# Experts' last product in three parts, with its weights split by VectorE

## The chip, the cores and the metric

The kernel runs on one core of a Trainium2 chip. The metric is the device time of one execution in microseconds (us), as the median of several runs. Engines are named as in the profile: PE (TensorE), PEld (its weight loads), DVE (VectorE), ACT (ScalarE), POOL (GpSimd), SP (SyncE, which here only issues DMAs).

## The reference

One transformer block on 2048 tokens of width 1024: a mixer of three kinds of attention, a mixture of experts, a gated embedding, and a norm. The change touches the last two.

```
def expert_block(inp):                      # one block of 128 tokens, one of 32 experts
    xb, e = inp
    hmid = jax.nn.silu(xb @ w_gate[e]) * (xb @ w_up[e])      # 1024 -> 512
    return hmid @ w_down[e]                                  # 512 -> 1024
...
h = h + hier_moe(rms_norm(h, g_ffn[i]), ...)
e = rms_norm(p[i] @ w_ple[i], g_ple[i])
h = h + e * jax.nn.sigmoid(h @ w_ple_gate[i])                # 1024 -> 1024
return rms_norm(h, g_final)
```

Each token goes to two experts. The tokens of an expert are padded to blocks of 128, so that an expert has one or more blocks; with these inputs 48 blocks are computed.

## The kernel before

The stages follow one another, each in a block of its own that starts when all engines have finished the one before: projections and the choice of keys, the mixers, the output product, routing (`route`), the experts (`experts`), and the last part (`finish`). All are written out by hand: each engine has its own list of instructions, in order, and waits on semaphores.

**Experts.** Every weight matrix of an expert is 2 MB, and one DMA loads it. Gate and up weights have two places (`low`, by the parity of the expert), and so have the down weights (`wd`). Gate and up products are made in three parts: a float32 matrix is split into `high`, its value cast to the type fp32r, and `low`, the rest, and PE adds high·high, high·low and low·high, three matmuls of 128x512 for each of the 8 slices of the inner dimension (L2361 to L2363). DVE makes the weights' parts, by halves of 128x2048: a cast (L2269) and a subtraction (L2271), so 4 pairs for an expert. `high` has one place for the gate and one for the up weights, so DVE's gate pairs of the next expert wait for the last gate product of this one (`g_done`), its up pairs for the last up product (`u_done`). POOL subtracts to make the low part of the turned input (`split_x`, L2296), ACT its high part (L2421). The down product (L2379) takes plain float32 operands, 8 matmuls of 128x512 per block, and each shows as two records.

PE's order in the loop, for block b: gate product of b+1, turning of the hidden values of b (`turn_h`, L2370), up product of b+1, turning of the input of b+2 (`turn_x`, L2349), down product of b (L2379). Below, these are G, H, U, X and Y. ACT: silu of b+1, copy of the turned hidden values of b (`copy_h`, L2439), copy of up, copies of the turned input, output of b. POOL: the gather of the input of b+2 (L2287, L2288), its list of rows (L2281), the product silu x up (`hidden`, L2302), the two subtractions of `split_x`. SP, for expert e from 2 on: wait for the last G of e-2, load gate (L2165); wait for the last U, load up; wait for the last Y, load down (L2170). The next expert's gate load stands behind that in SP's order.

**The last part.** While the experts run, SP loads the gate weights of the last part into a place of their own (`wg`) and DVE casts them into `low`'s even place once its expert pairs are done (L2275). When `finish` begins, DVE first subtracts to get their low part (L2765, 8 instructions), then adds the experts' results to h (L2727) and makes the low part of the turned h (L2736). ACT first squares and copies the embeddings of the first three tiles (L2681, L2683), then copies the turned h (L2690). PE turns and multiplies those embeddings (L2627, L2637), turns h (L2615) and makes the gate product in three parts (L2651 to L2653) for 16 tiles.

Of the kernel before, what the change touches and what calls it, by code (L numbers as in the profile page):

```python
# [1859 lines left out]
def route(nc, outer, router, slots, gates, rows, blocks, ident, prefetch, p, w_ple, room, e_dram, e_squares, f_dram, xb, x_loaded):  # L1860
# [5 lines left out]
    with ExitStack() as ctx:  # L1866
# [38 lines left out]
        emb, pt = room[:, 0:4, :], room[:, 4:8, :].rearrange("p a (b n) -> p (a b) n", n=PLE)  # L1905
# [247 lines left out]
GATE, UP = 0, 1  # L2153


def expert_weights(nc, outer, low, wd):
# [3 lines left out]
    return low, wd, gu_loaded, outer.enter_context(nc.semaphore("p7_d_loaded"))  # L2160
# [19 lines left out]
def experts(nc, outer, f_dram, weights, w_gate, w_up, w_down, gathers, y_dram, blocks, ident, load_next, load_tail, wg, wg_high, wg_loaded):
# [3 lines left out]
    with ExitStack() as ctx:  # L2186
# [9 lines left out]
        low, wd, gu_loaded, d_loaded = weights  # L2196
# [22 lines left out]
        hT_turned, hT_done = sem("hT_turned"), sem("hT_done")  # L2219
# [10 lines left out]
        def _(sp):  # L2230
# [26 lines left out]
        def _(dve):  # L2257
            with dve.Fori(0, NE // 2) as it:
                for par in range(2):
# [3 lines left out]
                    for m, done in ((GATE, g_done), (UP, u_done)):  # L2263
                        dve.wait_ge(gu_loaded[m][par], it * 16 + 16)

                        dve.wait_ge(done, once)
                        for half in range(2):
                            k = slice(half * HK, (half + 1) * HK)
                            dve.tensor_copy(high[:, m, k, :], low[:, par, m, k, :].bitcast(F32)).then_inc(high_done, 1)  # L2269
                            dve.wait_ge(high_done, e * 4 + (2 * m + half + 1))  # L2270
                            dve.tensor_tensor(low[:, par, m, k, :], low[:, par, m, k, :].bitcast(F32), high[:, m, k, :].bitcast(F32), ALU.subtract).then_inc(w_split, 1)  # L2271

            for k in range(KD):
                dve.wait_ge(wg_loaded, 16 * KD)
                dve.tensor_copy(wg_high[:, k, :], wg[:, k, :]).then_inc(wg_split, 1)  # L2275
            dve.wait_ge(wg_split, KD)

        @block.gpsimd
        def _(pool):
# [18 lines left out]
            def hidden(b, par):  # L2298
# [3 lines left out]
                pool.tensor_tensor(hid[:, par, :], act_g[:, :], act_u[:, :], ALU.mult).then_inc(h_done, 1)  # L2302
# [7 lines left out]
            hidden(0, 0)  # L2310
            split_x(1)
            m = rounds(pool)
            with pool.Fori(0, m) as it:
                for par in range(2):
# [4 lines left out]
                    hidden(b + 1, 1 - par)  # L2319
                    split_x(b + 2)  # L2320
            hidden(m * 2 + 1, 1)
# [8 lines left out]
        def _(pe):  # L2330
# [35 lines left out]
            def turn_h(b, par):  # L2366
                pe.wait_ge(h_done, b + 1)
                pe.wait_ge(hT_done, b + 1)
                for k in range(KF):
                    mm = pe.transpose(psH[:, k * P:(k + 1) * P], hid[:, par, k * P:(k + 1) * P], ident[:, :])  # L2370
                mm.then_inc(hT_turned, 1)

            def down(b, par, e, at):
                pe.wait_ge(hT_done, b + 2)
                pe.wait_ge(d_loaded, e * 16 + 16)
                for c in range(2):
                    pe.wait_ge(y_copied[c], b + 1)
                    for k in range(KF):
                        mm = pe.matmul(psY[:, c, :], hT[:, par, k, :], wd[:, bass.ds(at, 1), k, c * CH:(c + 1) * CH].rearrange("p a f -> p (a f)"),  # L2379
                                       start=k == 0, stop=k == KF - 1)  # L2380
# [8 lines left out]
            with pe.Fori(0, m) as it:  # L2389
                for par in range(2):  # L2390
# [3 lines left out]
                    turn_h(b, par)  # L2394
# [3 lines left out]
                    down(b, par, e, at)  # L2398
# [3 lines left out]
            turn_h(b, 0)  # L2402
            product(b + 1, UP, e, at)
            e, at = expert(b)
            down(b, 0, e, at)
            turn_h(b + 1, 1)
            e, at = expert(b + 1)
            down(b + 1, 1, e, at)

        @block.scalar  # L2410
        def _(act):
# [24 lines left out]
            def copy_h(b, par):  # L2436
                act.wait_ge(hT_turned, b + 2)
                act.wait_ge(y_done, b * 2 + 2)
                act.activation(hT[:, par, :, :], psH[:, :].rearrange("p (k t) -> p k t", t=P), ACT.Copy).then_inc(hT_done, 1)  # L2439
# [15 lines left out]
            with act.Fori(0, m) as it:  # L2455
                for par in range(2):
                    b = it * 2 + par
                    silu(b + 1)
                    copy_h(b, par)
# [5 lines left out]
            copy_h(b, 0)  # L2465
            copy_u(b + 1)
            output(b, 0, m)
            copy_h(b + 1, 1)
# [3 lines left out]
def finish_weights(nc, outer, ctx):  # L2472
# [9 lines left out]
    wg, first_h = sb("p8_wg", [KD, D]), sb("p8_first_h", [D])  # L2482
    low, wd = sb("p7_low", [2, 2, KD, FE], F32R), sb("p7_wd", [2, FE // P, D])
    return (wg, first_h, low, wd), (sem("w_loaded"), sem("h_loaded0"), sem("tail_loaded"))


def split_places(weights):
    low = weights[0][2]
    return [low[:, i, :, :, :].rearrange("p m k f -> p (m k f)").rearrange("p (k n) -> p k n", n=D) for i in range(2)]


def tail_places(weights):

    wd = weights[0][3]
    return (wd[:, 0, 0:2, :], wd[:, 0, 2, 0:OWN * PLE].rearrange("p (j n) -> p j n", n=PLE), wd[:, 0, 3, :],
            wd[:, 1, 0, :], wd[:, 1, 1, :], wd[:, 1, 2, 0:2 * KP * P].rearrange("p (b k t) -> p b k t", b=2, k=KP))


def load_finish_weights(sp, weights, w_pg, h_dram):
    (wg, first_h, _, _), (w_loaded, h_loaded, _) = weights  # L2500
    for k in range(KD):
        sp.dma_start(wg[:, k, :], w_pg[0, k * P:(k + 1) * P, :]).then_inc(w_loaded, 16)
    sp.dma_start(first_h[:, :], h_dram[0:P, :]).then_inc(h_loaded, 16)


def load_tail(sp, weights, p, w_ple, g_ple):
    wp, ptail, gp, _, _, _ = tail_places(weights)
# [3 lines left out]
    sp.dma_start(gp, row_broadcast(g_ple, D)).then_inc(tail_loaded, 16)  # L2511
    sp.wait_ge(w_loaded, 16 * KD)
    sp.wait_ge(h_loaded, 16)
    sp.wait_ge(tail_loaded, 48)


def finish(nc, outer, h_dram, y_dram, rows, gates, e_dram, e_squares, weights, blocks, g_final, out, ident):

    with ExitStack() as ctx:  # L2519
# [7 lines left out]
        (wg, first_h, low_gu, _), (_, h_loaded0, _) = weights  # L2527
        wg_high, wg_low = split_places(weights)
        wp, ptail, gp, second_h, gf, pT = tail_places(weights)
        ht = [first_h[:, :], second_h]  # L2530
        half = sb("half", [P, 1])
        e, y1, y2 = sb("e", [P, NS, D]), sb("y1", [P, NS, D]), sb("y2", [P, NS, D])
        hT_high, hT_low = sb("hT_high", [P, 2, KD, P], F32R), sb("hT_low", [P, 2, KD, P], F32R)

        sg, result, junk = wg[:, 0:2, :], wg[:, 2:4, :], wg[:, 4, :]
# [22 lines left out]
        def _(sp):  # L2558
# [9 lines left out]
            load_h(1)  # L2568
            load_h(2)
# [38 lines left out]
        def _(pe):  # L2608
# [11 lines left out]
            second = pe.snap((first + 1) % 2)  # L2620
# [19 lines left out]
            def product(t, halves=(0, 1)):  # L2640
# [5 lines left out]
                for c in halves:  # L2646
                    for k in range(KD):
                        if (t, c) == (0, 0):
                            pe.wait_ge(w_split, k + 1)
                        w_high, w_low = (low_gu[:, bass.ds(i, 1), k // 4, k % 4 * 2 + c, :].rearrange("p a f -> p (a f)") for i in (first, second))  # L2650
# [66 lines left out]
        def _(dve):  # L2717
# [46 lines left out]
            for k in range(KD):  # L2764
# [17 lines left out]
def hybrid_block_kernel(nc, x, p, rel_bias, g_mix, w_in, gla_w_alpha, gla_b_alpha, gla_g_norm, swa_sinks, w_out, g_ffn,  # L2782
# [14 lines left out]
    with ExitStack() as outer:  # L2797
# [17 lines left out]
        with ExitStack() as ctx:  # L2815
            ple = finish_weights(nc, outer, ctx)
            (wg, _, low, wd), (wg_loaded, _, _) = ple
            with ExitStack() as ffn:
                weights = expert_weights(nc, outer, low, wd)
                gathers = first_gathers(nc, outer, ffn, router)  # L2820

                def prefetch(sp, e_copied):
# [8 lines left out]
                route(nc, outer, router, gathers[0], gates, rows, blocks, ident, prefetch, p, w_ple, wg, e_dram, e_squares, f_dram, gathers[1], gathers[2])  # L2831
                experts(nc, outer, f_dram, weights, w_expert_gate, w_expert_up, w_expert_down, gathers, y_dram, blocks, ident,
                        lambda sp: load_finish_weights(sp, ple, w_ple_gate, h_dram), lambda sp: load_tail(sp, ple, p, w_ple, g_ple),
                        wg, split_places(ple)[0], wg_loaded)
            finish(nc, outer, h_dram, y_dram, rows, gates, e_dram, e_squares, ple, blocks, g_final, out, ident)
# [24 lines left out]
```

## Time and profile before

| | |
|---|---|
| three runs | 2977.5, 2985.3, 2990.5 us; median 2985.3 |
| the profiled execution | 2976.7 us, of which the span is 2975.0 us |
| routing ends, experts begin | at about 1771 us of the span |
| experts end, last part begins | 2746 to 2754 us |
| PE busy over the span | 2673.1 us (90%) |
| DVE busy | 1818.3 us (61%) |
| POOL busy | 952.3 us (32%) |

An engine's busy share is a mean over stages with different limits. Times in the trace are microseconds from the start of the span. The row of a timeline gives start, duration, engine, line, operation, tile written <- tiles read, how many are merged in the row, and in brackets how long the engine had been idle before and what ended that.

### The profile page before, as it was taken

What the parts mean: (1) busy time and instruction counts of PE and PEld (TensorE: products, weight loads), DVE (VectorE), ACT (ScalarE), POOL (GpSimd) and SP (SyncE); (2) the same over time, 40 slices, a digit from 0 to 9 for tenths busy, and PEclk for the clock granted to TensorE, in tenths of its full rate; (3) what the DMA queues carried; (4) which work ended last, traced back from release to release, by engine and by line L of the source; (5) the groups of instructions that cost most, each with busy time, mean ns of one, the idle gap of its engine ahead of it and who ended that gap; (6) DMA issues with size and microseconds to landing.
All of it is one profiled execution on the core that took longest, in us unless ns stands there. A gap on an engine that the chain in (4) does not pass through costs nothing. (4 is left out here: it accounts for less than half of the span.)

```text
span 2975.0 us, 34899 instructions
## 1 busy us (share of the span) xinstructions
PE 2673.1 (90%) x11088; PEld 1675.0 (56%) x11089; DVE 1818.3 (61%) x2274; ACT 1279.4 (43%) x2369; POOL 952.3 (32%) x935
## 2 busy tenths in 40 slices
PE   6989889999957878878799888999999999998998
PEld 3634333444843444444588746666666666665687
DVE  2187999688886756776322367764564445741676
ACT  2377878839805566665322142222222222222322
POOL 1477887200011111120000014543444334531321
PEclk9999999999977989999799899999999999999999
DMA  5102221111141122222544377996596655982563
GB/s 152 55 30 53 31 38 40 54 56 56 40 128 43 62 66 74 70 81 66 179 148 149 123 268 261 339 352 216 204 342 219 219 213 204 344 298 82 194 216 135
DMA packets 221746, 438.61 MB, mean 147 GB/s; under 512 B 23032, under 2 KB 91192, under 8 KB 221496
## 3 DMA queue, kind: packets, MB, share of 16 engines
q1 hardware_dynamic: 199384, 357.26, 35.0%
q0 software_dynamic: 13456, 47.85, 5.1%
q10 hardware_dynamic: 8784, 31.99, 2.6%
q8 instruction: 63, 1.03, 0.1%
q14 instruction: 59, 0.48, 0.0%
HBM read 331.14 MB, written 105.91 MB: 147 GB/s over the span
## 5 line engine op out<-in xcount | busy, mean ns | idle before, releaser
L2269 DVE CAST p_high<-p_low 128x2048 fp32r<-128x2048 f32 x128 | 203.1, 1587 | 407.6 <-PE p_psG L2363 292.8
L626 PE MATMUL p_psP<-home,p_ring 128*128 128x512 f32 (+1 forms) x960 | 420.6, 597 | 0.0
L2379 PE MATMUL p_psY<-p_wd,p_hT 128*128 x768 | 339.7, 596 | 2.2 <-ACT p_hT L2439 1.9
L2271 DVE TENSOR_TENSOR p_low<-p_low,p_high 128x2048 fp32r<-128x2048 f32 x128 | 319.9, 2499 | 4.4
L626 PEld LDWEIGHTS p_psP<-home,p_ring 128*128 128x128 f32 (+1 forms) x960 | 175.4, 185 | 239.6 <-issue 239.4
L2379 PEld LDWEIGHTS p_psY<-p_wd,p_hT 128*128 128x128 f32 x768 | 143.0, 191 | 164.8 <-issue 164.7
L2302 POOL TENSOR_TENSOR p_hid<-p_act_g,p_act_u 128x512 f32<-128x512 f32 x48 | 62.7, 1306 | 526.5 <-ACT p_act_u L2434 274.2
L2296 POOL TENSOR_TENSOR p_xT_low<-p_xT,p_xT_high 128x512 fp32r<-128x512 f32 x96 | 189.6, 1994 | 4.0 <-ACT p_xT L2424 4.0
L655 PE MATMUL p_psI<-p_kI,p_qI 64*128 64x512 f32 (+3 forms) x608 | 146.0, 587 | 48.7 <-ACT p_relu L551 48.5
L2361 PE MATMUL p_psG<-p_high,p_xT_high 128*128 128x512 f32 x384 | 170.2, 443 | 15.7 <-DVE p_low L2271 8.1
L699 DVE TENSOR_SCALAR_CACHE_REDUCE p_equal<-p_S_low,p_flip 128x512 uint8<-128x512 f32 (+4 forms) x139 | 168.7, 1213 | 0.0
L2361 PE MATMUL p_psU<-p_high,p_xT_high 128*128 128x512 f32 x384 | 157.8, 411 | 5.9 <-DVE p_low L2271 5.9
L565 ACT ACTIVATE p_relu<-p_relu,p_small 128x512 f32<-128x512 f32 (+3 forms) x266 | 161.5, 662 | 0.0
L2445 ACT ACTIVATE p_y<-p_psY 128x512 f32<-128x512 f32 x96 | 57.4, 598 | 226.7 <-PE p_psY L2379 226.7
L2362 PE MATMUL p_psG<-p_low,p_xT_high 128*128 x384 | 153.1, 399 | 0.0
L2363 PE MATMUL p_psG<-p_high,p_xT_low 128*128 128x512 f32 x384 | 152.8, 398 | 0.0
L551 ACT ACTIVATE p_relu<-p_psI 128x1024 f32<-128x1024 f32 (+3 forms) x152 | 136.7, 914 | 37.1 <-PE p_psI L655 12.6
L699 DVE TENSOR_SCALAR_CACHE_REDUCE p_above<-p_S_low,p_flip 128x384 uint8<-128x384 f32 (+4 forms) x139 | 150.6, 1083 | 3.3
L2362 PE MATMUL p_psU<-p_low,p_xT_high 128*128 x384 | 152.0, 396 | 0.0
L2363 PE MATMUL p_psU<-p_high,p_xT_low 128*128 128x512 f32 x384 | 151.9, 396 | 0.0
L1331 PE MATMUL p_psL<-p_kA,home 64*128 64x512 f32 (+3 forms) x320 | 86.6, 617 | 67.9 <-ACT home L1217 33.3
L1474 DVE SCALAR_TENSOR_TENSOR p_logits<-p_mask,p_psL 128x1024 f32<-128x1024 uint8 (+3 forms) x80 | 84.8, 1060 | 100.6 <-PE p_psL L1331 100.5
(397 smaller groups left out, 5592.7 us busy)
## 6 DMA issues: line engine op xcount, KB each, us to landing
p_low<-in_w_expert_gate_dram SPq DMA_DIRECT2D x32, 2048.0 KB, 13.5
p_low<-in_w_expert_up_dram SPq DMA_DIRECT2D x32, 2048.0 KB, 18.1
p_wd<-in_w_expert_down_dram SPq DMA_DIRECT2D x32, 2048.0 KB, 10.7
y_dram<-p_y ACTq DMA_DIRECT2D x48, 512.0 KB, 8.2
p_xt<-in_x_dram SPq DMA_DIRECT2D x32, 512.0 KB, 4.4
y_dram<-p_clear SPq DMA_DIRECT2D x32, 512.0 KB, 4.5
proj_f<-p_stage SPq DMA_DIRECT2D x52, 256.0 KB, 2.3
p_ot<-o_dram SPq DMA_DIRECT2D x16, 512.0 KB, 4.3
```

Of the source, the lines that this page charges most:

```text
L551: act.activation(relu[:, n % NRELU, :, 0:c1 - c0], psI[:, n % NI, :, 0:c1 - c0], ACT.Relu).then_inc(relu_done, 1)
L565: act.activation(dst, src, ACT.Copy, scale=small[:, j, h:h + 1]).then_inc(weighed, 1)
L626: mm = pe.matmul(psP[0:n, i % 2, :], w, aT[:, k, c * CH:(c + 1) * CH], start=k == 0, stop=k == KD - 1)
L655: mm = pe.matmul(psI[:, n % NI, half, 0:c1 - c0], qI[r, b % 2, i, :], kI[r, c0:c1], start=True, stop=True)
L699: return dve.tensor_scalar((above, equal)[jj % 2][:, 0:W], scores_of(S_low, S_high, j), value, None, ALU.is_ge, ALU.add, accum_out=cnt[:, ...
L2269: dve.tensor_copy(high[:, m, k, :], low[:, par, m, k, :].bitcast(F32)).then_inc(high_done, 1)
L2271: dve.tensor_tensor(low[:, par, m, k, :], low[:, par, m, k, :].bitcast(F32), high[:, m, k, :].bitcast(F32), ALU.subtract).then_inc(w_split, 1)
L2296: pool.tensor_tensor(xT_low[:, k, :], xT[:, k, :], xT_high[:, k, :].bitcast(F32), ALU.subtract).then_inc(xT_split, 1)
L2361: pe.matmul(ps[:, :], xT_high[:, k, :], high[:, m, k, :], start=k == 0, stop=False)
L2362: pe.matmul(ps[:, :], xT_high[:, k, :], left, start=False, stop=False)
L2363: mm = pe.matmul(ps[:, :], xT_low[:, k, :], high[:, m, k, :], start=False, stop=k == KD - 1)
L2379: mm = pe.matmul(psY[:, c, :], hT[:, par, k, :], wd[:, bass.ds(at, 1), k, c * CH:(c + 1) * CH].rearrange("p a f -> p (a f)"), start=k == 0 ...
```

## The change

The down product is made in three parts too. The down weights get a high and a low place for each parity (`down`, which takes the room of `wd` and of the last part's `wg`); DVE splits them after the up weights of the same expert. ACT writes the turned hidden values twice (`hT_high`, `hT`), POOL subtracts to get `hT_low` (`split_h`, ahead of `hidden` in its order), and Y waits for both splits. `hid`, `hT` have one place each instead of two, so `copy_h` of b waits for Y of b-1. The last part's gate weights are loaded in two halves into `low`'s even place when the last expert but one has left it, and DVE splits them there, into `down`'s even place and in place, after the last expert's weights; `finish` no longer subtracts. Its other tiles move into the odd places; g_ple is loaded at the start of `finish`. In routing, the first down load goes ahead of the second expert's gate load.

```diff
@@ load_down @@
-    sp.dma_start(wd[:, par, :, :], ...).then_inc(d_loaded, 16)
+    sp.dma_start(down[:, par, LOW_PART, :, :].bitcast(F32), ...).then_inc(d_loaded, 16)
@@ experts: sync @@
-            load_next(sp)
...
-            twice = sp.snap(used * 2 + 4)
-            sp.wait_ge(y_done, twice)
+            once = sp.snap(used + 1)
+            for m, done in ((GATE, g_done), (UP, u_done)):
+                sp.wait_ge(done, once)
+                sp.wait_ge(w_split, 4 * (NE - 2) + 2 * m + 2)
+                load_gate_half(sp, m)
+            used = sp.value_load(blocks[0:1, NBX + 2 + NE:NBX + 3 + NE], min_val=0, max_val=NBLK)
+            once = sp.snap(used + 1)
+            sp.wait_ge(u_done, once)
             load_tail(sp)
@@ experts: vector, after the gate and up pairs of expert e @@
+                    dve.wait_ge(d_loaded, e * 16 + 16)
+                    for half in range(2):
+                        k = slice(half * KF // 2, (half + 1) * KF // 2)
+                        dve.tensor_copy(down_w[:, par, HIGH, k, :], down_w[:, par, LOW_PART, k, :].bitcast(F32)).then_inc(d_high, 1)
+                        dve.wait_ge(d_high, e * 2 + (half + 1))
+                        dve.tensor_tensor(down_w[:, par, LOW_PART, k, :], down_w[:, par, LOW_PART, k, :].bitcast(F32), down_w[:, par, HIGH, k, :].bitcast(F32), ALU.subtract).then_inc(d_split, 1)
+            dve.wait_ge(y_done, twice)
             for k in range(KD):
-                dve.wait_ge(wg_loaded, 16 * KD)
-                dve.tensor_copy(wg_high[:, k, :], wg[:, k, :]).then_inc(wg_split, 1)
+                dve.wait_ge(wg_loaded, 16 * 2)
+                dve.tensor_copy(wg_high[:, k, :], wg[:, k, :].bitcast(F32)).then_inc(wg_split, 1)
+                dve.wait_ge(wg_split, 2 * k + 1)
+                dve.tensor_tensor(wg[:, k, :], wg[:, k, :].bitcast(F32), wg_high[:, k, :].bitcast(F32), ALU.subtract).then_inc(wg_split, 1)
@@ experts: gpsimd @@
+            def split_h(b):
+                pool.wait_ge(hT_done, b + 2)
+                pool.tensor_tensor(hT_low[:, :, :], hT[:, :, :], hT_high[:, :, :].bitcast(F32), ALU.subtract).then_inc(hT_split, 1)
...
-                pool.wait_ge(hT_turned, b)
+                pool.wait_ge(hT_turned, b + 1)
...
                     load_slots(b + 3, 1 - par)
-                    hidden(b + 1, 1 - par)
+                    split_h(b)
+                    hidden(b + 1)
                     split_x(b + 2)
@@ experts: tensor, down @@
-                pe.wait_ge(hT_done, b + 2)
-                pe.wait_ge(d_loaded, e * 16 + 16)
+                pe.wait_ge(hT_split, b + 1)
+                pe.wait_ge(d_split, e * 2 + 2)
...
-                        mm = pe.matmul(psY[:, c, :], hT[:, par, k, :], wd[...], start=k == 0, stop=k == KF - 1)
+                        pe.matmul(psY[:, c, :], hT_high[:, k, :], w_high, start=k == 0, stop=False)
+                        pe.matmul(psY[:, c, :], hT_high[:, k, :], w_low, start=False, stop=False)
+                        mm = pe.matmul(psY[:, c, :], hT_low[:, k, :], w_high, start=False, stop=k == KF - 1)
@@ experts: scalar, copy_h @@
-                act.wait_ge(y_done, b * 2 + 2)
-                act.activation(hT[:, par, :, :], psH[...], ACT.Copy).then_inc(hT_done, 1)
+                act.wait_ge(y_done, b * 2 + 4)
+                act.activation(hT_high[:, :, :], src, ACT.Copy)
+                act.activation(hT[:, :, :], src, ACT.Copy).then_inc(hT_done, 1)
@@ finish: sync, vector @@
+            sp.dma_start(gp, row_broadcast(g_ple, D)).then_inc(gp_loaded, 16)
...
-            for k in range(KD):
-                dve.tensor_tensor(wg_low[:, k, :], wg[:, k, :], wg_high[:, k, :].bitcast(F32), ALU.subtract).then_inc(w_split, 1)
             add(0)
             low(0)
             add(1)
+            dve.wait_ge(gp_loaded, 16)
@@ prefetch, in routing @@
-                    for e in range(2):
-                        load_gate_up(sp, weights, GATE, e, e, w_expert_gate)
-                        if e == 1:
-                            sp.wait_ge(e_copied, NT - OWN - 4)
-                        load_gate_up(sp, weights, UP, e, e, w_expert_up)
-                    load_down(sp, weights, 0, 0, w_expert_down)
+                load_gate_up(sp, weights, GATE, 0, 0, w_expert_gate)
+                load_gate_up(sp, weights, UP, 0, 0, w_expert_up)
+                load_down(sp, weights, 0, 0, w_expert_down)
+                sp.wait_ge(e_copied, NT - OWN - 4)
+                load_gate_up(sp, weights, GATE, 1, 1, w_expert_gate)
+                load_gate_up(sp, weights, UP, 1, 1, w_expert_up)
```

## Rows read from the trace of the kernel before

**Rows 1.** Busy by stretch: stretch, length, PE, PEld, DVE, ACT, POOL, clock, DMA, GB/s.
```profile
1771.00:2750.00 979.00, 949.86 (x3648) 639.30 (x3648) 519.94 (x264) 234.59 (x433) 421.98 (x282) 0.99 0.69 252
1790.00:1800.00 10.00, 4.94 (x20) 3.92 (x19) 9.93 (x5) 2.56 (x5) 9.21 (x4) 0.83 0.69 240
```

**Rows 2.** Waits, 1771 to 2750: waiting, awaited, total us, times, longest.
```profile
DVE p_high L2269 <- PE p_psG L2363: 292.8, 16, 21.7
DVE p_high L2269 <- DMA p_low<-in_w_expert_gate_dram: 97.7, 13, 14.2
```

**Rows 3.** Timeline of PE in a two-block expert: H, U, Y, G, H.
```profile
2403.61 0.60 PE L2370 MATMUL p_psH<-ident,p_hid 128*128 128x128 f32 x4
...
2410.52 7.03 PE L2379 MATMUL p_psY<-p_wd,p_hT 128*128 x16
2416.99 0.79 PE L2361 MATMUL p_psG<-p_high,p_xT_high 128*128 128x512 f32 x1
2417.62 0.40 PE L2362 MATMUL p_psG<-p_low,p_xT_high 128*128 x1
...
2422.97 0.60 PE L2370 MATMUL p_psH<-ident,p_hid 128*128 128x128 f32 x4
```

**Rows 4.** Timeline of DVE: the pairs of expert 10, the first of expert 11.
```profile
1992.66 1.23 DVE L2269 CAST p_high<-p_low 128x2048 fp32r<-128x2048 f32 x1 [16.49 <-PE p_psG L2363]
...
1996.13 1.22 DVE L2269 CAST p_high<-p_low 128x2048 fp32r<-128x2048 f32 x1
...
1999.59 2.29 DVE L2269 CAST p_high<-p_low 128x2048 fp32r<-128x2048 f32 x1
2001.91 3.24 DVE L2271 TENSOR_TENSOR p_low<-p_low,p_high 128x2048 fp32r<-128x2048 f32 x1
...
2007.40 2.29 DVE L2271 TENSOR_TENSOR p_low<-p_low,p_high 128x2048 fp32r<-128x2048 f32 x1
2031.39 1.23 DVE L2269 CAST p_high<-p_low 128x2048 fp32r<-128x2048 f32 x1 [21.70 <-PE p_psG L2363]
```

**Rows 5.** Timeline of DVE: first casts of experts 0, 9, 13, 17, 24, 30.
```profile
1770.94 1.23 DVE L2269 CAST p_high<-p_low 128x2048 fp32r<-128x2048 f32 x1 [17.09 <-issue]
...
1961.07 1.43 DVE L2269 CAST p_high<-p_low 128x2048 fp32r<-128x2048 f32 x1 [6.03 <-DMA p_low<-in_w_expert_gate_dram]
...
2108.86 1.23 DVE L2269 CAST p_high<-p_low 128x2048 fp32r<-128x2048 f32 x1 [21.70 <-PE p_psG L2363]
...
2210.14 1.23 DVE L2269 CAST p_high<-p_low 128x2048 fp32r<-128x2048 f32 x1 [16.49 <-PE p_psG L2363]
...
2481.28 1.23 DVE L2269 CAST p_high<-p_low 128x2048 fp32r<-128x2048 f32 x1 [21.69 <-PE p_psG L2363]
...
2625.07 1.23 DVE L2269 CAST p_high<-p_low 128x2048 fp32r<-128x2048 f32 x1 [16.49 <-PE p_psG L2363]
```

**Rows 6.** Timeline of SP's queue, and of DVE: a down load; a later gate landing.
```profile
1880.90 0.37 SPq L2170 DMA_DIRECT2D p_wd<-in_w_expert_down_dram  x1
...
1897.08 1.89 DVE L2269 CAST p_high<-p_low 128x2048 fp32r<-128x2048 f32 x1 [5.66 <-DMA p_low<-in_w_expert_gate_dram]
```

**Rows 7.** Timeline of POOL beside the pairs of rows 4.
```profile
1999.42 1.37 POOL L2302 TENSOR_TENSOR p_hid<-p_act_g,p_act_u 128x512 f32<-128x512 f32 x1 [14.05 <-issue]
2000.76 5.52 POOL L2296 TENSOR_TENSOR p_xT_low<-p_xT,p_xT_high 128x512 fp32r<-128x512 f32 x2
...
2007.56 3.02 POOL L2288 DMA_INDIRECT p_xb<-f_dram,p_slot  x1 [0.15 <-issue]
```

**Rows 8.** Timeline of PE, after the longest idle gap within the experts.
```profile
1795.95 0.62 PE L2361 MATMUL p_psG<-p_high,p_xT_high 128*128 128x512 f32 x1 [5.06 <-POOL p_xT_low L2296]
```

**Rows 9.** Timelines of DVE and ACT, start of the last part.
```profile
2754.03 9.17 DVE L2765 TENSOR_TENSOR p_low<-p_wg,p_low 128x1024 fp32r<-128x1024 f32 x8 [68.20 <-PEq L2186]
...
2764.47 1.28 DVE L2727 SCALAR_TENSOR_TENSOR p_hs<-p_y,gates,p_first_h 128x1024 f32<-128x1024 f32 x1
...
2770.17 1.08 ACT L2690 ACTIVATE p_hT_high<-p_psT 128x512 fp32r<-128x512 f32 x2
```

More of the change, by code:

```diff
@@ L2309, in _ @@
             split_x(0)
-            hidden(0, 0)
+            hidden(0)
             split_x(1)
@@ L2318, in _ @@
                     load_slots(b + 3, 1 - par)
-                    hidden(b + 1, 1 - par)
+                    split_h(b)
+                    hidden(b + 1)
                     split_x(b + 2)
-            hidden(m * 2 + 1, 1)
+            split_h(m * 2)
+            hidden(m * 2 + 1)
+            split_h(m * 2 + 1)
             for par in range(2):
@@ L2397, in _ @@
                     e, at = expert(b)
-                    down(b, par, e, at)
+                    down(b, e, at)
             b = m * 2
@@ L2458, in _ @@
                     silu(b + 1)
-                    copy_h(b, par)
+                    copy_h(b)
                     copy_u(b + 1)
@@ L2480, in sb, with gate_places, load_gate_half, load_tail @@
         return ctx.enter_context(nc.sbuf_tensor(name, [P, *shape], dt))
[L2482 to L2489, printed above, removed]
-def tail_places(weights):
[L2494 to L2500, printed above, removed]
-    for k in range(KD):
[L2502 to L2507, printed above, removed]
+    first_h = sb("p8_first_h", [D])
+    low, down = sb("p7_low", [2, 2, KD, FE], F32R), sb("p7_down", [2, 2, FE // P, D], F32R)
+    xb, xT = sb("p7_xb", [2, D]), sb("p7_xT", [KD, P])
+    return (first_h, low, down, xb, xT), (sem("w_loaded"), sem("h_loaded0"), sem("tail_loaded"))
+def gate_places(weights):
+    _, low, down, _, _ = weights[0]
+    return low[:, 0, :, :, :].rearrange("p m k f -> p (m k f)").rearrange("p (k n) -> p k n", n=D), down[:, 0, :, :, :].rearrange("p a k n -> p (a k) n")
+def tail_places(weights):
+    _, _, _, xb, xT = weights[0]
+    return xb[:, :, :], xT[:, 0:OWN * PLE // P, :].rearrange("p k t -> p (k t)").rearrange("p (j n) -> p j n", n=PLE)
+def load_gate_half(sp, weights, m, w_pg):
+    half = slice(m * KD // 2, (m + 1) * KD // 2)
+    sp.dma_start(gate_places(weights)[0][:, half, :].bitcast(F32), w_pg[0, m * D // 2:(m + 1) * D // 2, :].rearrange("(k p) n -> p k n", p=P)).then_inc(weights[1][0], 16)
+def load_tail(sp, weights, p, w_ple, h_dram):
+    wp, ptail = tail_places(weights)
     _, (w_loaded, h_loaded, tail_loaded) = weights
@@ L2510, in load_tail, with finish @@
     sp.dma_start(ptail, p[0, 0, 0:OWN * P, :].rearrange("(j p) n -> p j n", p=P)).then_inc(tail_loaded, 16)
-    sp.dma_start(gp, row_broadcast(g_ple, D)).then_inc(tail_loaded, 16)
-    sp.wait_ge(w_loaded, 16 * KD)
+    sp.dma_start(weights[0][0][:, :], h_dram[0:P, :]).then_inc(h_loaded, 16)
+    sp.wait_ge(w_loaded, 32)
     sp.wait_ge(h_loaded, 16)
-    sp.wait_ge(tail_loaded, 48)
-def finish(nc, outer, h_dram, y_dram, rows, gates, e_dram, e_squares, weights, blocks, g_final, out, ident):
+    sp.wait_ge(tail_loaded, 32)
+def finish(nc, outer, h_dram, y_dram, rows, gates, e_dram, e_squares, weights, blocks, g_ple, g_final, out, ident):
     with ExitStack() as ctx:
@@ L2835, in hybrid_block_kernel, with prefetch @@
-            finish(nc, outer, h_dram, y_dram, rows, gates, e_dram, e_squares, ple, blocks, g_final, out, ident)
+            (_, low, down, xb, xT), (wg_loaded, _, _) = ple
+            weights = expert_weights(nc, outer, low, down)
+            gathers = first_gathers(nc, outer, xb, router)
+            def prefetch(sp, e_copied):
+                load_gate_up(sp, weights, GATE, 0, 0, w_expert_gate)
[4 more added lines that the diff above has]
+                load_gate_up(sp, weights, UP, 1, 1, w_expert_up)
@@ new lines, in hybrid_block_kernel @@
+            room = [down[:, i, HIGH, :, :].bitcast(F32) for i in range(2)]
+            route(nc, outer, router, gathers[0], gates, rows, blocks, ident, prefetch, p, w_ple, room, e_dram, e_squares, f_dram, gathers[1], gathers[2])
+            experts(nc, outer, f_dram, weights, w_expert_gate, w_expert_up, w_expert_down, gathers, y_dram, blocks, ident, xT,
+                    lambda sp, m: load_gate_half(sp, ple, m, w_ple_gate), lambda sp: load_tail(sp, ple, p, w_ple, h_dram), *gate_places(ple), wg_loaded)
@@ L2839 @@
+            finish(nc, outer, h_dram, y_dram, rows, gates, e_dram, e_squares, ple, blocks, g_ple, g_final, out, ident)
 _INS = ['x', 'p', 'rel_bias', 'g_mix', 'w_in', 'gla_w_alpha', 'gla_b_alpha', 'gla_g_norm', 'swa_sinks', 'w_out', 'g_ffn',
```

94 lines of the change are left out of this document (42 added, 52 removed).

## The prediction

> **What bounds the kernel now.** I read the busy times by stretch first: in the experts, 979 us of the span, PE is busy 950 us, at full clock; DVE is busy 520 us and POOL 422 us, so DVE looks half free [rows 1]. The waits correct that: DVE waits 292.8 us for the last gate product, 16 times, and 97.7 us for gate weights, 13 times [rows 2]. These are two regimes. So I then went through DVE's timeline for the first cast of every expert, T below, and what each had waited for [rows 4 to 6]. Neighbours are 38.7 us apart (1992.66 to 2031.39 [rows 4]) or about 21 us: two blocks or one. Counted through, experts 0 to 8, 13 to 15 and 24 to 28 have one block (17), experts 9 to 12, 16 to 23, 29 and 30 have two (14), and 31 has three: 17 + 28 + 3 = 48.
>
> With two blocks PE never stops: a block takes 2422.97 - 2403.61 = 19.36 us [rows 3], and DVE idles 21.7 of 38.7 us [rows 4]. With one block, gate weights are late: a down load goes out at 1880.90 and the gate load behind it has landed at 1897.08, 16.2 us later [rows 6]. I take the lengths of the runs as they stand [rows 4, 5]: T(0) to T(9) 190.1 us, T(9) to T(10) 31.6, T(10) to T(13) 116.2, T(13) to T(17) 101.3, T(17) to T(24) 271.1, T(24) to T(30) 143.8.
>
> **PE's gain.** Y takes 2416.99 - 2410.52 = 6.47 us to the start of G, and G's first matmul then 0.63 us to the next start, where the other 23 steps take (2422.97 - 2417.62) / 23 = 0.233 us each [rows 3]. So Y really costs 6.47 + 0.40 = 6.87 us. In three parts it is 24 x 0.233 = 5.6 us, and 0.1 us for standing behind a turning in float32, as U does behind H. That is 1.16 us less per block, 18.2 instead of 19.36 us. Over 48 blocks it would be 56 us, if PE set the pace everywhere.
>
> **DVE's new work.** Two more pairs per expert. A free pair takes 1996.13 - 1992.66 = 3.47 us, so two take 6.9 us, and all six 20.8 us. Beside POOL they are slower: the cast of 1999.59 takes 2.29 us instead of 1.22, the subtraction after it 3.24 where the free one takes 2.2 (3.47 less the cast). The four pairs of this expert last until 2009.69, 17.03 us instead of 13.87, while POOL runs three full-size operations [rows 4, 7]: 1.06 us for each. `split_h` makes it four per block, 4.2 us. So an expert with one block needs D = 20.8 + 4.2 = 25.0 us of DVE. PE needs 18.2. The load loop needs less too: in such a turn Y of the expert before ends 24.2 us after T (below), plus 16.2 us to a landed gate makes 40.4 us for two turns, against 50. Hence DVE becomes the bound in every one-block expert. Ends of D: 24.0, if the new POOL operation falls where DVE doesn't feel it, and 26.5, if the descriptors and one-element operations of POOL begin to cost; I take 25.0, which is the three measured ones and a fourth alike.
>
> The Trainium skill (SBUF — State Buffer, section "Who interferes with whom") speaks against the change: a DVE cast in a two-port mode, or a DVE operation with two inputs in SBUF, and a GpSimd operation that reads SBUF exclude each other for a whole instruction. By that rule the added splits of the two engines collide in full, as the 4.2 us have it; without it D would be 20.8. The trace agrees with it, by 1.22 against 2.29 us.
>
> **The sum, after minus before.** In a one-block run T moves by D.
> - Experts 0 to 8: expert 0 takes 13.9 + 6.9 us for its pairs and about 3.6 beside POOL, so T(1) = 1795.3; expert 1 takes 25.3, with POOL's backlog, so T(2) = 1820.6; seven more at 25.0 give T(9) = 1995.6 against 1961.07: +34.5.
> - T(9) to T(10), where a second block follows a DVE-bound turn. After T, G's second half waits for two pairs (6.9) and takes 2.8: 9.7. U's second half waits for four pairs and one POOL operation (14.9): 17.7. X and Y end at 24.2, the second G at 29.8. Against 31.6: -1.8.
> - T(13) to T(17): three turns of 25.0 and one of 29.8 make 104.8, against 101.3: +3.5. T(24) to T(30): five and one, 154.8 against 143.8: +11.0.
> - Two-block experts 10 to 12, 17 to 23 and 30: 11 x 2 x 1.16 = -25.5. DVE's 25.0 us fit into 36.4.
> - Expert 31: five Y gain 5.8; behind the last H stands nothing but Y, so ACT's second copy and `split_h` lie open (0.6 + 1.3 us, an estimate from the durations of a 128x512 operation on each): net -3.8.
> - Together 34.5 - 1.8 + 3.5 + 11.0 - 25.5 - 3.8 = +17.9.
> - Clock. In a DVE-bound turn PE is idle from 24.2 to 28.6 us after T, 4.4 us. The trace has one such gap, 5.06 us: the G behind it begins with matmuls of 0.62 us instead of 0.40 [rows 8], in a stretch with a granted clock of 0.83, a mixture of the 1.2 and 2.4 GHz levels [rows 1], and loses about 9 x 0.2 = 1.8 us of which a part is the gap's own. Within a one-block run PE has 6.8 us to spare and this is hidden; where a two-block expert follows (9, 16, 29) up to 1.8 us is not. I take +2 in all, between 0 and 5.
>
> **The rest, at nothing.** In routing the order of loads changes, but 6 MB go ahead of the wait and 4 MB behind it as now, and the first down load is early. ACT's second copy lies beside U. `copy_h` of b now waits for Y of b-1, which ended before G. `split_h` stands behind gather and list and ahead of `hidden` on POOL, and Y needs it 6.9 us after H's start [rows 3]; it takes some 1.6 us on ACT and 1.3 to 3 us on POOL. If that cover goes, Y waits: the third rival. The last part's gate pairs (8 of half size, about 15 us) start when Y of expert 30 is over and lie under two blocks of expert 31; their loads go out a block earlier. `finish` loses 9.17 us of DVE, but its first addition ends at 2765.75 and ACT, busy with embeddings, copies h at 2770.17 [rows 9]: those 9.17 us hid already, so 0, at best -1. g_ple's broadcast is issued with the first loads of `finish` and is used after that copy; if it were late, embedding(0) waits, a few us once.
>
> So +20 us on the profiled execution's own 2976.7: 2996.7 us. That execution lies 8.6 us under the median of the runs, 2985.3, so for the runs I predict 3005 us.
>
> **Rivals.**
> - PE's gain prevails (faster). If POOL's operations cost a DVE that never rests less than 1.06 us, and the casts keep their pace, D is nearer 22. Three us less in 17 turns: 20 - 51 = -31, 2954 us. For it: few stretches of the trace have DVE busy without pause. Against: in those each POOL operation cost the full 1.06 us. Chance 0.15.
> - Offset. D = 24.0 to 24.5 and no loss to the clock: 20 - 2 - 17 x 0.75 = +5, 2990 us. For it: D rests on a count of POOL operations, and some may fall on waits. Chance 0.25.
> - POOL becomes late (slower still). Beside a busy DVE, from `hidden` to the end of the descriptors POOL takes 2010.58 - 1999.42 = 11.2 us [rows 7], and `split_h` then up to 2.8 (half of 5.52): 14 us, where Y is due some 17 us after `hidden` in a two-block run. It decides from 3 us of further delay; at 1 us in each of the 31 blocks outside one-block runs the time is 3005 + 31 = 3036. Against: DVE rests in a third of a two-block expert, and POOL is quick then. Chance 0.12.
> - The forecast, DVE-bound at 25 us: 0.48; its own range 2990 to 3022.
>
> A difference under 0.5% (15 us) is about what a measurement of this kernel can't tell from none. Slower by more: the forecast without its part under 3000 (0.40), late POOL 0.12, the upper edge of the offset case 0.03: 0.55. Within: 0.08 + 0.21 = 0.29. Faster by more: 0.15 and the lower edge of the offset case, 0.16. The range 2970 to 3036 leaves out most of the first rival and half of the third.
>
> **What would show it.** In the profile after: first casts 25 us apart in one-block runs, DVE without a pause there; 36.4 us apart in two-block runs; 24 starts 0.233 us apart in Y; DVE busy 520 + 32 x 6.9 + 48 x 1.06 = 792 us in the experts, and the gate's 8 subtractions besides; PE idle some 4 us before G in one-block turns, waiting for DVE. The forecast is wrong if those casts are under 23.8 us apart (17 x 1.2 us eats the 20), or if PE waits at Y for `hT_low`.

## The result, and the profile after

The changed kernel takes 3014.9 us (median of 4 runs, 3012.6 to 3019.6) against 2983.1 us before: ratio 1.0104, 95% interval 1.0087 to 1.0121. It is slower by some 32 us (31 by the ratio); 20 were forecast. The profiled execution took 3019.57 us, with a span of 3017.9 us.

Busy time by stretch, answering to [rows 1]: the experts but for their last 18 us, the turn of expert 5 (one block), and 72 us of two-block experts (columns as there).
```profile
1787.47:2770.00 982.53, 896.57 (x3982) 720.79 (x3983) 832.94 (x400) 253.93 (x475) 652.62 (x328) 0.96 0.68 248
1911.86:1935.79 23.93, 19.19 (x79) 15.50 (x80) 23.72 (x14) 4.94 (x10) 13.51 (x7) 0.86 0.84 307
2078.00:2150.00 72.00, 72.00 (x336) 58.70 (x335) 52.35 (x24) 21.37 (x40) 51.14 (x28) 1.00 0.62 231
```
In the one-block turn DVE is busy 23.72 of 23.93 us and PE's granted clock is 0.86; in two-block turns PE never stops. The waits of the whole stage (1771 to 2800), answering to [rows 2]:
```profile
DVE p_high L2276 <- PE p_psG L2389: 127.9, 14, 9.8
PE p_psG L2387 <- DVE p_low L2278: 81.5, 19, 9.5
PE p_psY L2406 <- POOL p_hT_low L2319: 3.7, 1, 3.7
```
DVE's waits for gate weights are gone, and PE now waits for DVE. PE waits for `split_h` once in the whole stage. DVE's timeline, the first casts of experts 0, 9, 13, 17, 24 and 30, answering to [rows 5]:
```profile
1787.47 1.23 DVE L2276 CAST p_high<-p_low 128x2048 fp32r<-128x2048 f32 x1 [17.46 <-issue]
...
2010.71 2.31 DVE L2276 CAST p_high<-p_low 128x2048 fp32r<-128x2048 f32 x1
...
2150.61 1.23 DVE L2276 CAST p_high<-p_low 128x2048 fp32r<-128x2048 f32 x1 [9.84 <-PE p_psG L2389]
...
2260.25 1.23 DVE L2276 CAST p_high<-p_low 128x2048 fp32r<-128x2048 f32 x1 [7.20 <-PE p_psG L2389]
...
2513.79 1.23 DVE L2276 CAST p_high<-p_low 128x2048 fp32r<-128x2048 f32 x1 [9.85 <-PE p_psG L2389]
...
2673.33 1.23 DVE L2276 CAST p_high<-p_low 128x2048 fp32r<-128x2048 f32 x1 [7.22 <-PE p_psG L2389]
```
The cast of expert 9 has no bracket: DVE went straight on from the expert before. One such turn on DVE, that of expert 5, answering to [rows 4]:
```profile
1911.86 2.28 DVE L2276 CAST p_high<-p_low 128x2048 fp32r<-128x2048 f32 x1
1914.17 2.29 DVE L2278 TENSOR_TENSOR p_low<-p_low,p_high 128x2048 fp32r<-128x2048 f32 x1
1916.38 1.22 DVE L2276 CAST p_high<-p_low 128x2048 fp32r<-128x2048 f32 x1
...
1926.77 2.33 DVE L2282 CAST p_down<-p_down 128x2048 fp32r<-128x2048 f32 x1
...
1932.59 3.27 DVE L2284 TENSOR_TENSOR p_down<-p_down 128x2048 fp32r<-128x2048 f32 x1
1935.79 2.31 DVE L2276 CAST p_high<-p_low 128x2048 fp32r<-128x2048 f32 x1
```
and POOL's full-size operations beside it, answering to [rows 7]:
```profile
1926.60 1.41 POOL L2319 TENSOR_TENSOR p_hT_low<-p_hT,p_hT_high 128x512 fp32r<-128x512 f32 x1 [6.64 <-ACT p_hT L2469]
1931.63 2.08 POOL L2325 TENSOR_TENSOR p_hid<-p_act_g,p_act_u 128x512 f32<-128x512 f32 x1 [3.62 <-issue]
1933.68 5.54 POOL L2315 TENSOR_TENSOR p_xT_low<-p_xT,p_xT_high 128x512 fp32r<-128x512 f32 x2
```
`split_h` runs from 1926.60, and the cast beside it takes 2.33 us instead of 1.22. This turn has three lengthened operations and takes 23.9 us; the next has five and takes 26.0. PE in a two-block expert, answering to [rows 3]: H, Y, G, H.
```profile
2404.93 0.60 PE L2396 MATMUL p_psH<-ident,p_hid 128*128 128x128 f32 x4
...
2411.76 0.48 PE L2406 MATMUL p_psY<-p_down,p_hT_high 128*128 x1
...
2417.44 0.40 PE L2387 MATMUL p_psG<-p_high,p_xT_high 128*128 128x512 f32 x1
2417.67 0.40 PE L2388 MATMUL p_psG<-p_low,p_xT_high 128*128 x1
...
2423.04 0.60 PE L2396 MATMUL p_psH<-ident,p_hid 128*128 128x128 f32 x4
```
Y takes 5.68 us and G's first step 0.23 us again; a block takes 18.11 us, was 19.36.

### The profile page after: what moved, and what is told of

The parts are those of the page before. It is cut to its first block and busy times, and to the rows that moved or that the text cites. A ratio compares the mean times of both kernels' runs of the same rounds, so it can differ in the third digit from the quotient of the medians.

```text
span 3017.9 us, 36375 instructions
## 1 busy us (share of the span) xinstructions
PE 2650.2 (88%) x11472; PEld 1773.3 (59%) x11473; DVE 2120.7 (70%) x2402; ACT 1303.7 (43%) x2417; POOL 1181.8 (39%) x983
## 3 DMA queue, kind: packets, MB, share of 16 engines
q1 hardware_dynamic: 199288, 357.26, 34.5%
q8 instruction: 64, 1.05, 0.1%
## 5 line engine op out<-in xcount | busy, mean ns | idle before, releaser
L2276 DVE CAST p_high<-p_low 128x2048 fp32r<-128x2048 f32 x128 | 223.6, 1747 | 145.3 <-PE p_psG L2389 127.9
L2315 POOL TENSOR_TENSOR p_xT_low<-p_xT,p_xT_high 128x512 fp32r<-128x512 f32 x96 | 225.3, 2367 | 3.4 <-ACT p_xT L2452 3.4
L2458 ACT ACTIVATE p_act_g<-p_psG 128x512 f32<-128x512 f32 x48 | 28.8, 599 | 358.8 <-PE p_psG L2389 358.8
L2319 POOL TENSOR_TENSOR p_hT_low<-p_hT,p_hT_high 128x512 fp32r<-128x512 f32 x48 | 99.5, 2074 | 198.4 <-ACT p_hT L2469 198.4
L2284 DVE TENSOR_TENSOR p_down<-p_down 128x2048 fp32r<-128x2048 f32 x64 | 165.2, 2581 | 2.2
L2388 PE MATMUL p_psG<-p_low,p_xT_high 128*128 x384 | 163.6, 426 | 0.0
L2389 PE MATMUL p_psG<-p_high,p_xT_low 128*128 128x512 f32 x384 | 163.0, 424 | 0.0
L2406 PE MATMUL p_psY<-p_down,p_hT_high 128*128 x384 | 157.2, 409 | 3.7 <-POOL p_hT_low L2319 3.7
L2325 POOL TENSOR_TENSOR p_hid<-p_act_g,p_act_u 128x512 f32<-128x512 f32 x48 | 109.1, 2273 | 128.2 <-issue 111.5
L2407 PE MATMUL p_psY<-p_down,p_hT_high 128*128 x384 | 152.8, 398 | 0.0
L2408 PE MATMUL p_psY<-p_down,p_hT_low 128*128 x384 | 152.7, 398 | 0.0
```

The source lines that it names most:

```text
L2284: dve.tensor_tensor(down_w[:, par, LOW_PART, k, :], down_w[:, par, LOW_PART, k, :].bitcast(F32), down_w[:, par, HIGH, k, :].bitcast(F32), ...
L2315: pool.tensor_tensor(xT_low[:, k, :], xT[:, k, :], xT_high[:, k, :].bitcast(F32), ALU.subtract).then_inc(xT_split, 1)
L2388: pe.matmul(ps[:, :], xT_high[:, k, :], left, start=False, stop=False)
L2389: mm = pe.matmul(ps[:, :], xT_low[:, k, :], high[:, m, k, :], start=False, stop=k == KD - 1)
L2406: pe.matmul(psY[:, c, :], hT_high[:, k, :], w_high, start=k == 0, stop=False)
L2407: pe.matmul(psY[:, c, :], hT_high[:, k, :], w_low, start=False, stop=False)
```

## The experiments

The theory: DVE became the bound in one-block experts (two pairs more and a fourth POOL operation beside it), and PE's gain shows only in the other blocks. The first four kernels take the change apart. Most differences are under 2%, so each ratio stands with its 95% interval; the profiles add the lengths of turns, which repeat more closely (223.24 and 223.25 us for the same nine turns in two profiles).

**The last part alone.**
```diff
-  # DVE: the two down pairs;  POOL: split_h;  ACT: the copy to hT_high
-  pe.matmul(..., hT_high[:, k, :], w_high, ...)  # and two more
+  mm = pe.matmul(psY[:, c, :], hT[:, k, :], w, start=k == 0, stop=k == KF - 1)  # w: the loaded weights as float32
```


> The changed kernel with its down product as before (float32, one part: no down pairs on DVE, no split_h on POOL, one copy on ACT). What is left of the change is the last part's gate weights, split as one more expert, and the new places and order of loads. Theory (DVE became the bound in one-block experts, the rest is worth nothing): first casts as in the kernel before, about 21 us apart in one-block runs and 38.7 in two-block runs, time equal to before within 5 us. Rival (the moved tiles, the load order or the last part's start carry part of the loss): 5 us or more above before. Second rival (the 9 us of subtractions that left finish were on the path): about 9 us below before.

2984.7 us, ratio 0.9995 (0.9980 to 1.0009). The first casts of experts 0 and 9 are 190.3 us apart and those of two-block runs 38.7 us, as before. Places, load order, the single place for the turned hidden values and the last part's split together are worth nothing that shows: the interval, -6 to +3 us, leaves out both rivals (+5 and -9). The 9 us taken out of `finish` had been hidden.

**DVE's pairs back.**
```diff
+  dve.tensor_copy(down_w[:, par, HIGH, k, :], down_w[:, par, LOW_PART, k, :].bitcast(F32))
+  dve.tensor_tensor(down_w[:, par, HIGH, k, :], ..LOW_PART.., ..HIGH.., ALU.subtract)   # in both halves
```


> The first one with DVE's two down pairs per expert put back; the subtraction writes over the high part, so that the float32 product can go on reading the loaded weights. Theory: with three POOL operations per block a one-block turn needs 20.8 + 3 x 1.06 = 24.0 us of DVE, so first casts are 24.0 us apart in one-block runs, 38.7 in two-block runs; nine turns to expert 9 take 214 us instead of 190, all 17 together cost about 40 us: 3022 us. Rival (DVE's work hides, the loss comes from POOL's new operation or the new waits): within 10 us of before.

3022.5 us, ratio 1.0120 (1.0103 to 1.0137): 3022 were expected, and the rival is out.

**POOL's `split_h` and ACT's copy back.**
```diff
+  act.activation(hT_high[:, :, :], src, ACT.Copy)
+  pool.tensor_tensor(hT_low[:, :, :], hT[:, :, :], hT_high[:, :, :].bitcast(F32), ALU.subtract).then_inc(hT_split, 1)
```


> The second one with ACT's second copy and POOL's split_h put back as well; the down product stays float32 in one part and waits for both splits. Theory: one more POOL operation per block costs a busy DVE 1.0 us, so first casts 25 us apart in one-block runs, unchanged in two-block runs: 17 us more than the second, about 3039 us. Rival (POOL's chain itself is late): PE waits at the down product for split_h, two-block runs grow above 38.7 us too.

3044.4 us, ratio 1.0191 (1.0172 to 1.0210). Its two-block runs stayed at 38.7 us, so POOL wasn't late. It is 22 us above the second one, where 17 were expected: in the two profiles 15.6 us of that lie between the first casts of experts 0 and 31 and 3.9 behind, where the last block waits for `split_h`; the rest lies ahead of the experts. The first casts of experts 0 and 9, with the pairs and then with the pairs and `split_h`:
```profile
1775.74 1.23 DVE L2276 CAST p_high<-p_low 128x2048 fp32r<-128x2048 f32 x1 [17.29 <-issue]
...
1989.64 2.29 DVE L2276 CAST p_high<-p_low 128x2048 fp32r<-128x2048 f32 x1
```
```profile
1784.51 1.23 DVE L2276 CAST p_high<-p_low 128x2048 fp32r<-128x2048 f32 x1 [17.47 <-issue]
...
2007.54 2.28 DVE L2276 CAST p_high<-p_low 128x2048 fp32r<-128x2048 f32 x1
```
That is 213.9 and 223.0 us for nine turns: 23.8 and 24.8 us each, hence 1.0 us of DVE's time for one POOL operation per block (with ACT's copy, which came back together with it). The kernel with everything, product in three parts included, has 223.2 us there: PE's gain is worth nothing in these turns.

**The product in three parts without DVE's pairs.**
```diff
-  # DVE: the two down pairs
-  for part in (HIGH, LOW_PART)
+  for part in (LOW_PART, LOW_PART)
```


> The changed kernel without DVE's two down pairs: the three matmuls of each step read the unsplit weights, so the splitting of the down weights is left out. It shows what the product in three parts gains by itself. Theory: two-block experts as in the changed kernel, 36.2 us; one-block runs go by the load loop, shortened by the quicker down product, about 20.4 us a turn: 28 us and 10 us less than before, and some 4 elsewhere: 2941 us. Rival (POOL's fourth operation or the single place for the turned hidden values also limits): one-block turns at 22 us or more, time above 2960.

This kernel leaves out the splitting of the down weights, so its time stands for the product alone and is no result of the whole block.

2942.8 us, ratio 0.9865 (0.9841 to 0.9889): the PE side alone is worth 1.35%, some 40 us, and 2941 us were expected. Two-block runs are at 36.2 us; one-block runs fell only from 190.3 to 187.6 us over nine turns, 20.8 us each, less than half of what was expected there, so the total came out right with one of its parts too large; DVE still waits some 5 us a turn for gate weights.

**Parts of the product.** If the cost has a knee, where DVE passes the load loop's 21 us, and the gain has none, a smaller share of the split should win. The first one, two or three of the four slices are split, the rest stays float32:
```diff
+  k = slice(0, SK)                       # SK = 2, 1 or 3; one DVE pair per expert, of 128 x SK*1024
...
+  if k >= SK:
+      mm = pe.matmul(psY[:, c, :], hT[:, k, :], w, start=k == 0, stop=k == KF - 1)
+      continue
```


> Half of the down product in three parts: of its four slices of the inner dimension the first two are split (one DVE pair per expert instead of two, split_h on POOL on half the size, ACT's high copy too), the other two stay float32. Theory: DVE needs 24.9 - 3.5 - 0.5 = 21 us in a one-block turn, no more than the load loop took before (21), so one-block runs cost nothing; a block of a two-block run takes 19.36 - 0.6 = 18.7 us, first casts 37.5 us apart. Sum -19 us from 31 blocks, and up to +8 in one-block runs: 2970 us, faster than both kernels. Rival (a mixed accumulation costs PE more at the changes of type than it saves, or one-block runs are DVE-bound above 22 us): 2985 or more.

2970.4 us, ratio 0.9956 (0.9942 to 0.9970): faster than both kernels. Its first casts of experts 6, 7, 18 and 19:
```profile
1903.78 1.74 DVE L2277 CAST p_high<-p_low 128x2048 fp32r<-128x2048 f32 x1 [1.74 <-DMA p_low<-in_w_expert_gate_dram]
...
1924.63 1.44 DVE L2277 CAST p_high<-p_low 128x2048 fp32r<-128x2048 f32 x1 [1.37 <-DMA p_low<-in_w_expert_gate_dram]
...
2248.85 1.23 DVE L2277 CAST p_high<-p_low 128x2048 fp32r<-128x2048 f32 x1 [16.34 <-PE p_psG L2389]
...
2286.30 1.23 DVE L2277 CAST p_high<-p_low 128x2048 fp32r<-128x2048 f32 x1 [16.34 <-PE p_psG L2389]
```
In the one-block run DVE waits for the load again, by 1.3 to 2.0 us at experts 4 to 9 (before, it was 5.7 to 6.4 at experts 5 to 9), so the added pair has filled most of the gap; a two-block turn is 37.45 us, 1.28 us less than before.

> A quarter: only the first slice is split (DVE pair of 128x1024). Theory: DVE needs about 19.5 us in a one-block turn, well under the load loop, so one-block turns stay at about 21 us; a block of a two-block run takes 19.36 - 0.3 = 19.05 us, first casts 38.1 apart: -10 us, about 2976 us. Rival (the fourth POOL operation and the wait for it cost at any size): no gain, 2984.

2976.7 us, ratio 0.9971 (0.9959 to 0.9983): the smaller gain, as forecast.

> Three quarters: three slices are split in one DVE pair of 128x3072, the fourth stays float32. Theory: DVE needs about 24.9 - 1.9 = 23 us in a one-block turn, 2 us over the load loop, 17 x 2 = +34 us; a block elsewhere gains 0.9 us, 31 x 0.9 = -28: about 2990 us, near before. Rival (gain and cost go in proportion to the share split, with no knee): 2983 + 0.75 x 32 = 3007.

2984.2 us, ratio 0.9997 (0.9983 to 1.0012). Nine turns take 203.85 us (22.65 each), two-block turns 36.8 us. By shares 0, 1/4, 1/2, 3/4, 1 the ratio runs 0.9995, 0.9971, 0.9956, 0.9997 and 1.0080 to 1.0104. It falls to the half and rises behind it: a knee, and no proportion. The intervals of quarter and half overlap. From the first cast to the end of the span, which leaves out where the experts begin, the profiles give 1203.0, 1190.8, 1187.2, 1199.7 and 1230.4 us. The product in three parts alone took 37.2 us off this stretch (1165.8 us). If a share of the split brings its share of that, an estimate of what DVE's pairs cost is -3, 3, 25 and 65 us: nearly nothing up to the half and steep from there. The partial kernels split by one long pair instead of two, so they also have fewer operations on DVE; that part isn't told apart.

**Where the experts begin.** No code was changed.

> The changed kernel once more, for where its first expert begins. In the profiles so far the stages ahead, whose work no kernel here changes, end with the first cast at 1771 to 1776 us of the span in five and at 1784 to 1787 us in four. Theory (that place is each execution's own and has nothing to do with the change): it may come out either way, and from that cast on the times are as in the first profile of the changed kernel, within 1 us: 223 us to expert 9, 36.2 us in two-block runs, 922 us to expert 31. Rival (the changed kernel always begins its experts late): 1784 us or later again, and all times at 3012 us or above.

3009.1 us, ratio 1.0080 (1.0063 to 1.0097). The first casts of experts 0 and 9:
```profile
1777.65 1.23 DVE L2276 CAST p_high<-p_low 128x2048 fp32r<-128x2048 f32 x1 [17.57 <-issue]
...
2000.90 2.31 DVE L2276 CAST p_high<-p_low 128x2048 fp32r<-128x2048 f32 x1
```
The beginning is 9.8 us earlier than in the first profile, the nine turns take 223.25 us against 223.24, expert 31 comes 922.0 us after expert 0 against 922.1, and the execution takes 3009.75 us against 3019.57. So what differs between the two profiles lies ahead of the experts, and the traces show where. In the mixers the same copy of L1251 begins at 1196.85 and 1196.74 us, 0.1 us apart; when the output product has begun, the same copy of L1787 begins at 1483.20 and 1473.16, 10.0 us apart. The stretch in which they part, and two groups of PE's matmuls in it, in the first profile and then in the second:
```profile
1230.00:1420.00 190.00, 156.14 (x874) 86.21 (x874) 122.18 (x178) 104.98 (x254) 30.57 (x36) 0.87 0.21 66
1234.05 1.11 PE L1342 MATMUL p_psX<-ident,p_logits 128*128 128x128 f32 x4 [1.14 <-ACT p_logits L1234]
1238.69 2.08 PE L1376 MATMUL p_psL<-home 64*128 64x256 f32 x8 [0.47 <-DVE p_logits L1474]
```
```profile
1230.00:1420.00 190.00, 150.12 (x902) 83.76 (x901) 130.56 (x188) 112.06 (x270) 37.75 (x40) 0.96 0.21 67
1233.96 0.66 PE L1342 MATMUL p_psX<-ident,p_logits 128*128 128x128 f32 x4 [1.34 <-ACT p_logits L1234]
1237.19 1.13 PE L1376 MATMUL p_psL<-home 64*128 64x256 f32 x8 [0.94 <-DVE p_logits L1474]
```
Up to 1232 us PE's gaps were alike (0.56 and 0.76 us against 0.56 and 0.77). Then its clock fell in the first profile, to 0.50 between 1235 and 1240 us, where it was 1.00 in the second; the matmuls of L1376 took 2.08 and 1.13 us. Over the whole stretch it was 0.87 and 0.96. The ten profiles fall into the same two groups: here the granted clock is 0.94 to 0.96 in the six that begin their experts early and 0.87 to 0.90 in the four that begin them late.

## Why the prediction was right

It held in sign, mechanism and range: 3005 us forecast, 3014.9 and 3009.1 measured. By its own steps, from first cast to first cast, the profile after minus the one before:

| step | forecast | measured |
|---|---|---|
| experts 0 to 8, one block each | +34.5 | +33.1 (223.2 against 190.1) |
| T(9) to T(10) | -1.8 | -0.3 |
| T(13) to T(17) | +3.5 | +8.4 |
| T(24) to T(30) | +11.0 | +15.8 |
| the eleven two-block experts | -25.5 | -27.7 |
| expert 31 and the last part | -3.8 | -2.9 |
| clock (in the rows above when measured) | +2 | |
| sum | +20 | +26.4 |

Two figures of the prediction are off in the last digit by its own terms: 3.16 us for three operations are 1.05 each, and expert 31 comes to -3.9. Neither changes the forecast.

- **D, right.** From T(1) to T(9), 1811.22 to 2010.71, a turn took 24.94 us, forecast 25.0. It is a mean: single turns took 23.9, 25.0 or 26.0 us, as three, four or five of DVE's operations were lengthened. Both terms were shown apart: two pairs and three POOL operations 23.8, the fourth 1.0 us.
- **PE's gain, right, forecast a little small.** A block took 18.11 us instead of 18.2: a gain of 1.25 us, forecast 1.16.
- **D taken as one size, the term that failed.** Experts 13 and 14, and 24 and 25, took 26.3 and 27.1 us. They stand behind a two-block run, and PE is not yet held back by DVE as in a settled turn. So the blocks come quicker than DVE's turns, and more than one block's POOL work falls into one of them; `split_h` begins 20.0, 19.6 and 25.9 us apart:
```profile
2152.30 3.01 POOL L2319 TENSOR_TENSOR p_hT_low<-p_hT,p_hT_high 128x512 fp32r<-128x512 f32 x1 [6.37 <-ACT p_hT L2469]
...
2172.28 1.29 POOL L2319 TENSOR_TENSOR p_hT_low<-p_hT,p_hT_high 128x512 fp32r<-128x512 f32 x1
...
2191.92 3.24 POOL L2319 TENSOR_TENSOR p_hT_low<-p_hT,p_hT_high 128x512 fp32r<-128x512 f32 x1 [1.33 <-ACT p_hT L2469]
...
2217.86 2.31 POOL L2319 TENSOR_TENSOR p_hT_low<-p_hT,p_hT_high 128x512 fp32r<-128x512 f32 x1 [5.72 <-ACT p_hT L2469]
```
  In the turn of expert 14 on DVE:
```profile
2176.91 2.32 DVE L2276 CAST p_high<-p_low 128x2048 fp32r<-128x2048 f32 x1
2179.26 3.26 DVE L2278 TENSOR_TENSOR p_low<-p_low,p_high 128x2048 fp32r<-128x2048 f32 x1
2182.45 2.31 DVE L2276 CAST p_high<-p_low 128x2048 fp32r<-128x2048 f32 x1
...
2193.93 2.32 DVE L2282 CAST p_down<-p_down 128x2048 fp32r<-128x2048 f32 x1
...
2198.49 2.32 DVE L2282 CAST p_down<-p_down 128x2048 fp32r<-128x2048 f32 x1
2200.85 3.26 DVE L2284 TENSOR_TENSOR p_down<-p_down 128x2048 fp32r<-128x2048 f32 x1
```
  Six lengthened operations, where a settled turn has four on average: 20.8 + 6 x 1.05 = 27.1 us. Each of the two pairs of turns is 3.4 us longer than D = 25.0 gives: 6.8 of the 9.7 us by which these two rows of the table were missed. The turns of experts 16 and 29, 31.2 us instead of 29.8, carry the rest; they are like the next.
- **T(9) to T(10), the rest.** G should have ended 9.7 us after T; it ended at 13.1. The first pair was slowed by POOL, so G began at 5.7, behind 4.08 us of idling. Its first four matmuls still took 0.40 to 0.50 us; then they took 0.63, and the granted clock of the stretch is 0.77, a mixture of the 1.2 and 2.4 GHz levels:
```profile
2016.42 0.50 PE L2387 MATMUL p_psG<-p_high,p_xT_high 128*128 128x512 f32 x1 [4.08 <-DVE p_low L2278]
...
2017.46 0.63 PE L2388 MATMUL p_psG<-p_low,p_xT_high 128*128 x1
```
  G took 7.24 us to H instead of 5.6. But little of that reached the turn's length, 31.3 us against 29.8. The last up pair now had two of POOL's operations ahead of it, not one, and its last operation was this one:
```profile
2024.38 2.29 DVE L2278 TENSOR_TENSOR p_low<-p_low,p_high 128x2048 fp32r<-128x2048 f32 x1
```
  It ended 16.0 us after T (forecast 14.9), and U's second half takes 2.8 us from there, to 2029.5; U ended at 2029.7. So by these rows the price of the low clock here is about 0.2 us, an estimate, where the prediction had up to 1.8 at each of three such places and 2 in all. The clock term was put in the right place but too large; the rest of the turn's 1.5 us is mainly the second lengthened operation. That the low clock within one-block runs is hidden agrees with D, which is DVE's time alone, at a granted clock of 0.86 on PE.
- **The edits costed at nothing were at nothing** (the last part alone, 0.9995), among them DVE's 9.17 us at the start of the last part. With the whole change `split_h` lies open once, behind the last H, as forecast: PE idles 3.7 us there (before, 1.9 us for ACT's copy).
- **DVE's busy time, too small.** The prediction had 792 us in the experts and the 8 subtractions besides; 833 were measured. It counted one operation more per block, 51 us. But in the kernel before 72 of DVE's full-size operations were lengthened, by 74 us in all, and now 144, by 154 us: POOL's other operations, part of which had run while DVE waited, now lie beside a busy DVE too. D had this right for one-block turns, by counting all four; the sum for the whole stage didn't.
- **What lies outside the forecast.** In the profile after, expert 0 begins 16.5 us later than in the one before; together with the 26.4 us this makes the 42.9 us between the spans. Ahead of it the two kernels differ only in routing's loads and places, and there the last part alone has the same (0.9995). Ten profiles begin their experts at 1771 to 1778 us (six) or 1784 to 1787 us (four), and the changed kernel itself is in both groups, so this isn't the change's. Some 10 us of it arise between 1230 and 1420 us, with PE's lower clock there. Of the rest some 5 us arise before 460 us, where the clock was 0.97 in the kernel before (360 to 460 us) and 0.90 to 0.93 in the nine others. Why the clock is lower in one execution than in another stays open. The forecast for the runs, 3005 us, took the profiled execution's distance from the median of the kernel before, 8.6 us, as that of the changed kernel; the stretch behind the first cast is the cleaner test, and there +20 stands against +26.4.

## What to carry to other kernels

Before moving work to an engine that looks half free, cut its busy time by turns of the loop: DVE's 53% in the experts was 15 of 21 us in short turns and 17 of 38.7 in long ones, and the short ones had 6 us to spare where the change wanted 10: 6.9 for the pairs, 1 for the new POOL operation, and 2 for POOL's old operations, which had run while DVE waited. Cost the contention of every full-size operation of GpSimd beside a busy VectorE, the old ones too, and not just the new operation itself. And where a change gains in proportion but costs only from a knee on, do a part of it: half of this one is 0.44% faster, all of it 0.8 to 1.0% slower.

## What the runs showed of the hardware

Each 128x512 operation of POOL beside a busy DVE cost DVE 1.0 us (213.9 to 223.0 us over nine turns), whose own operations have four times the elements. By the Trainium skill (SBUF — State Buffer, section "Who interferes with whom") the two engines share one pair of ports, which a VectorE instruction in a two-port mode takes for its whole length and one with two inputs in SBUF needs for the second. The runs agree with this, and give the price: casts went from 1.22 to some 2.3 us, subtractions from 2.29 to some 3.25. A mixed accumulation of fp32r and float32 matmuls in one PSUM tile cost PE nothing visible: the quarter, half and three-quarters splits brought 0.32, 0.64 and 0.96 us a block, of 1.25 for the whole.

Two executions of one kernel came to differ by 10 us within 190 us of the mixers: with PE's gaps alike to 0.1 us up to 1232 us of the span, its granted clock from there to 1420 us was 0.87 in one and 0.96 in the other.
